# Encoder layer on one core: copies of the turned probabilities spread over two engines, a reordered handover from the output projection to gate/up, and a split low part in down

## The chip, the cores and the metric

The kernel runs on one core of a Trainium2 chip. The metric is the device time of the whole program in microseconds (us); smaller is better. A core has TensorE (PE, matrix products; its weight loads are shown as PEld), VectorE (DVE), ScalarE (ACT), GpSimd (POOL) and SyncE (SP, which issues most DMAs). Each engine works through its own instructions strictly in order; between engines there are semaphores, on which an instruction waits until a count is reached.

## The reference

One layer of a streaming encoder, on 2048 prompt tokens and 8 streams of 16 new tokens (2176 tokens, 1024 wide):

```python
h = rmsnorm(x, norm_mix_pre)
qa, ka, va, logf, qb, kb, vb = project_in(h, w_in, b_forget)
oa = fox_fn(qa, ka, va, logf)          # 8 heads x 64, causal, bias C[t]-C[s]
ob = band_fn(qb, kb, vb)               # 8 heads x 64, own chunk and 8 before it
oa = rmsnorm(oa.reshape(...), gain_out_a)
ob = rmsnorm(ob.reshape(...), gain_out_b)
mix = jnp.concatenate([oa, ob], axis=-1) @ w_out
x = x + rmsnorm(mix, norm_mix_post)
hf = rmsnorm(x, norm_ffn_pre)
ff = (jax.nn.silu(hf @ w_gate) * (hf @ w_up)) @ w_down
x = x + rmsnorm(ff, norm_ffn_post)
```

`attend` inside both heads' functions is softmax(q k / 8 + bias) v.

## The kernel before

Every product with weights is done as three passes: both operands are split into a high part (a rounded copy, type fp32r, made on ACT) and a low part (original minus high, made on DVE or POOL), and PE adds high x high, high x low and low x high. So each operand costs an ACT and a DVE (or POOL) instruction before PE can use it. In names, a final h or l stands for these parts (`ffn_wh`, `ffn_wl`).

The stages follow each other on the one core: the front projections (to about 615 us), attention (615 to 1303), the output projection (1305 to 1535, 17 tiles of 128 tokens, NT = 17), gate and up (1544 to 2492), down (2492 to 3005) and a short tail. The order of each engine's work is written by hand.

**Attention.** PE computes scores (`att_s`, L1077), DVE adds the bias and reduces the row's extreme (L1353), ACT takes the exponential (`exps`, L1219, into `att_sx`), PE turns the probabilities by 64 x 64 transposes (`turn`, L1114 and L1094) into two PSUM banks `pt[0]` and `pt[1]` (both shown as `att_pt`), which are copied to SBUF (`att_pts`), and PE multiplies them with the values (L1152). There are 296 turns. There is one pair of `pt` banks for all of them, so a turn waits until both copies of the turn before are done: `copied(G - 1)` waits on `s_ca` (ACT's copies, L1230) and `s_cd` (DVE's, L1364). The first bank is always copied by ACT. The second is copied by ACT if the next turn comes behind value products (`LONG`, 176 turns: ACT makes both copies, one after the other) and by DVE if it comes right after (120 turns, called split turns here):

```python
def by_dve(G, x):
    return x == 1 and not LONG[G]
```

**The handover to gate/up.** The output projection's last two tiles (x = 15 and 16) pass through group sums (`group_b`, L1792), post-norm (`resid_add`, L1811 and L1817, which ends x1), the norm before gate/up (`second`, `hidden`) and a transpose (L1726) whose result DVE copies out (`mix_hidden`, L1800, `mix_ht`) and SP stores to `mid_hT`. Gate and up are then a Strassen-like product: 3 windows of tokens times 22 weight tiles (`n` from 0 to 65), each with 7 products (`product(n, x)`, x = 0 to 6, PE lines L2179, L2181, L2182) of sums of blocks. The first window's sums and parts are made during the handover: `ffn_sr` (three sums, L2466, L2472, L2486), `high_h(0, x)` on ACT (L2270) and `low_h(0, x)` on DVE (L2412) for x = 0 to 6. For each weight tile POOL makes four sums (`w_sums`, L2093 to L2099, into `ffn_tr`), ACT the high parts (`high_first` L2239, `high_sums` L2245, `high_lower` L2252, `high_up` L2257), DVE the low parts (`low_first` L2389, `low_sums` L2395, `low_lower` L2401, `low_up` L2405). Results meet in DVE's additions u2, u3, c22, c21, c12 (L2505 to L2549). Of what PE waits for: product 3 needs ACT's copy `p1` of product 0's result (`ffn_p`, L2341), product 5 needs u3, product 6 needs c22; product (1, 0) needs the copies of tile 16.

**Down.** 34 tiles; tile n needs `ah[n % 2]` (ACT, L2287) and `al[n % 2]`. Tile 0's low part is made in two halves side by side (POOL L2137, DVE L2511), tile 1's whole by POOL (L2140), the later ones whole by DVE (L2423). There is one landing buffer `ar` for all tiles, loaded by SP's `acts(n)`.

Of the kernel before, what the change touches and what calls it, by code (L numbers as in the profile page):

```python
# [7 lines left out]
ALU = mybir.AluOpType  # L8
# [649 lines left out]
def attend(nc, t, keep, neg_c, recips):  # L658
# [9 lines left out]
    DVES = counted(0 if x else 1 for x in LONG)  # L668
# [25 lines left out]
    with ExitStack() as ctx:  # L694
# [105 lines left out]
        with nc.Block() as block:  # L800
# [236 lines left out]
            def _(pe):  # L1037
# [154 lines left out]
            def _(act):  # L1192
# [29 lines left out]
                def copy(n, g, x):  # L1222
                    G = T0[n] + g
                    if by_dve(G, x):
                        return
# [24 lines left out]
            def _(dve):  # L1250
# [105 lines left out]
                def copy(n, g):  # L1356
                    G = T0[n] + g
                    if not by_dve(G, 1):
                        return
# [514 lines left out]
def output_and_ffn(nc, t, mix_sem, up, down, ahead, recips):  # L1874
# [9 lines left out]
    with ExitStack() as ctx:  # L1884
# [80 lines left out]
        with nc.Block() as block:  # L1965

            @block.sync
            def _(sp):
# [32 lines left out]
                def acts(n):  # L2001
                    if n >= NM:
                        return
                    sp.wait_ge(s_low, min(n, 2))
                    sp.wait_ge(s_al, max(n - 1, 1))
                    act_halves(n)
# [20 lines left out]
                for n in range(NU):  # L2027
# [56 lines left out]
            def _(pool):  # L2084
# [55 lines left out]
                nc.gpsimd.tensor_tensor(al[1][:], ar, f32(ah[1][:]), ALU.subtract).then_inc(s_low, 1)  # L2140
# [6 lines left out]
            def _(pe):  # L2147
# [51 lines left out]
                for n in range(NM):  # L2199
                    c, i = divmod(n, NT)  # L2200
                    u = n % 2
                    out = py[n % NPY][:]
                    if n == 1:
                        pe.wait_ge(s_low, 2)
                    else:
                        pe.wait_ge(s_al, max(n, 1))
# [25 lines left out]
            def _(act):  # L2232
# [95 lines left out]
                act.wait_ge(mix.s_x1, NT)  # L2328
                for n in range(NU):
# [5 lines left out]
                    high_first(n + 1)  # L2335
# [5 lines left out]
                    nc.scalar.activation(p1[:, :w], X[u][:, :w], ACT.Copy).then_inc(s_p1, 1)  # L2341
                    if NU - 6 <= n < NU - 2:
# [8 lines left out]
                    high_sums(n + 1)  # L2351
# [6 lines left out]
                    nc.scalar.activation(sg[:, :w], X[u][:, :w], ACT.Silu).then_inc(s_g1, 1)  # L2358
                    if n == NU - 1:
# [24 lines left out]
            def _(dve):  # L2384
# [74 lines left out]
                group_b(NT - 2, 1)  # L2459
                variance(NT - 1)  # L2460
                resid(NT - 2)
                resid_add(NT - 2)
# [3 lines left out]
                nc.vector.tensor_tensor(sr[:, 0, :, :w], a21, a22, ALU.add).then_inc(s_sd, 1)  # L2466
                group_b(NT - 1, 0)
                low_first(0)
                second(NT - 2)
                mix_hidden(NT - 3)  # L2470
                dve.wait_ge(s_sd, 1)
                nc.vector.tensor_tensor(sr[:, 1, :, :w], sr[:, 0, :, :w], a11, ALU.subtract).then_inc(s_sd, 1)  # L2472
                low_sums(0)
                group_b(NT - 1, 1)
                low_h(0, 0)
                resid(NT - 1)
# [4 lines left out]
                mix_hidden(NT - 2)  # L2481
                dve.wait_ge(mix.sth[1], 16 * len(range(1, NT, 2)))
                low_lower(0)
                low_h(0, 3)
                dve.wait_ge(s_sd, 2)
                nc.vector.tensor_tensor(sr[:, 2, :, :w], a12, sr[:, 1, :, :w], ALU.subtract).then_inc(s_sd, 1)  # L2486
                low_h(0, 4)
                low_h(0, 5)
                mix_hidden(NT - 1)
                low_h(0, 6)  # L2490
                dve.wait_ge(mix.st1[2], 16 * len(range(2, NT, 3)))
                dve.wait_ge(mix.s_h, NT - 2)
                dve.wait_ge(mix.s_th, NT - 1)
# [169 lines left out]
```

## Time and profile before

| | |
|---|---|
| three runs, median | 3031.85 us (3030.17 to 3039.38) |
| the profiled execution | 3030.77 us, of which the span of the trace is 3029.0 us |
| mean granted TensorE clock | 0.981 |
| busy: PE, PEld | 2847.1 us (94%), 2551.3 us (84%) |
| busy: DVE, ACT, POOL | 1632.7 us (54%), 1201.2 us (40%), 752.3 us (25%) |
| shares of the chain that ended last | PE 50%, DVE 3%, issue 1%, DMA 1%, ACT 1% |

PE is busy for 2847.1 of 3029.0 us, so at most some 180 us of idle PE can be won without less PE work; a busy share is a mean over stages with different limits, and what a wait is worth has to be read where it stands. In the rows below, a row of a timeline gives the start, the duration, the engine, the line, and in brackets the idle time ahead of the instruction and what ended it.

### The profile page before, as it was taken

Reading aid. Unit: us, or ns where it says so; the run is one execution under the profiler, and the core shown is the slowest. Engines: PE = TensorE matmul, PEld = TensorE weight load, DVE = VectorE, ACT = ScalarE, POOL = GpSimd, SP = SyncE. Lnnn points to the kernel's source line nnn. Section 1 sums busy time; section 2 is a strip of 40 time slices with the busy share of each in tenths; the row PEclk is TensorE's granted clock in tenths of the full one; section 3 lists DMA queues with packets and bytes.
Section 4 is the critical chain, followed back from the end, with each engine's and each line's share of the span. In section 5 each row is a group of like instructions: output and inputs, shape, how many; then the busy total and the mean of one; then the engine's idle time right before and its main releaser. Section 6 shows DMA issues by size and latency. Waiting matters only on the chain.

```text
span 3029.0 us, 54879 instructions
## 1 busy us (share of the span) xinstructions
PE 2847.1 (94%) x22143; PEld 2551.3 (84%) x22143; DVE 1632.7 (54%) x2945; ACT 1201.2 (40%) x2080; POOL 752.3 (25%) x683
## 2 busy tenths in 40 slices
PE   7999999979999789969979999999999999999998
PEld 7999999957777566758869999999999997887887
DVE  6222121166667456757777667776776662224443
ACT  5330000057777566745543334333433342223221
POOL 0000000055345123023335444543443420000000
PEclk9999999979999999989989999999999999999999
DMA  5322212152112897567723322423223345335553
GB/s 169 96 72 78 76 62 76 48 165 76 63 39 56 256 293 239 152 198 218 242 96 135 112 95 94 152 95 114 89 102 112 128 133 148 96 96 162 165 165 120
DMA packets 285540, 384.75 MB, mean 127 GB/s; under 512 B 24473, under 2 KB 211113, under 8 KB 273513
## 3 DMA queue, kind: packets, MB, share of 16 engines
q1 hardware_dynamic: 284984, 379.68, 39.9%
q8 instruction: 177, 2.90, 0.4%
q10 hardware_dynamic: 304, 1.57, 0.2%
q14 instruction: 75, 0.61, 0.1%
HBM read 291.91 MB, written 89.28 MB: 126 GB/s over the span
## 4 chain that ended last, share of the span: by engine, by line
PE 50%; DVE 3%; issue 1%; DMA 1%; ACT 1%; POOL 0%; SPq 0%; DVEq 0%; POOLq 0%; ACTq 0%
PE ffn_x L2179 3%; PE ffn_w L2179 3%; PE ffn_x L2182 3%; PE ffn_w L2182 3%; PE ffn_x L2181 3%; PE ffn_w L2181 3%; PE ffn_z L2179 3%; PE ffn_z L2182 3%; PE ffn_z L2181 3%; PE ffn_z L2214 1%; PE ffn_z L2216 1%; PE ffn_w L2214 1%; PE ffn_z L2215 1%; PE ffn_w L2216 1%; PE ffn_y L2179 1%
## 5 line engine op out<-in xcount | busy, mean ns | idle before, releaser
L1230 ACT ACTIVATE att_pts<-att_pt 128x384 f32<-128x384 f32 (+3 forms) x472 | 209.7, 483 | 203.9 <-PE att_pt L1114 190.1
L1219 ACT ACTIVATE att_sx<-att_sx,att_nm 128x640 f32<-128x640 f32 (+17 forms) x272 | 264.8, 980 | 6.4 <-DVE att_nm L1353 6.4
L1114 PEld LDWEIGHTS att_pt<-att_eye,att_sx 64*128 64x128 f32 x3296 | 130.7, 140 | 126.5 <-ACT att_pts L1230 66.4
L80 PE MATMUL frt_pz<-frt_xhi,frt_hi 128*128 128x448 f32 (+1 forms) x640 | 230.5, 360 | 0.0
L82 PE MATMUL frt_pz<-frt_xhi,frt_lo 128*128 128x448 f32 (+1 forms) x640 | 230.5, 360 | 0.0
L81 PE MATMUL frt_pz<-frt_xlo,frt_hi 128*128 128x448 f32 (+1 forms) x640 | 230.0, 359 | 0.0
L1114 PE MATMUL att_pt<-att_eye,att_sx 64*128 64x64 f32 x3296 | 168.9, 233 | 63.2 <-ACT att_pts L1230 23.0
L515 DVE TENSOR_TENSOR frt_shared<-frt_pz,frt_rb 128x448 f32<-128x448 f32 (+1 forms) x80 | 48.9, 612 | 313.5 <-PE frt_pz L82 313.5
L1152 PE MATMUL att_po<-att_pts,att_vv 128*64 128x128 f32 x3296 | 217.2, 279 | 0.0
L1152 PEld LDWEIGHTS att_po<-att_pts,att_vv 128*64 128x64 f32 x3296 | 177.9, 137 | 44.7 <-ACT att_pts L1230 25.9
L2179 PE MATMUL ffn_z<-ffn_hh,ffn_wh 128*128 128x362 f32 (+1 forms) x528 | 174.2, 330 | 3.6 <-DVE ffn_u L2515 3.4
L80 PE MATMUL frt_pv<-frt_hi,frt_xhi 128*128 128x256 f32 (+1 forms) x544 | 157.3, 289 | 18.7 <-DVE frt_lo L447 15.8
L2182 PE MATMUL ffn_z<-ffn_hh,ffn_wl 128*128 128x362 f32 (+1 forms) x528 | 173.7, 329 | 0.0
L2181 PE MATMUL ffn_z<-ffn_hl,ffn_wh 128*128 128x362 f32 (+1 forms) x528 | 173.0, 328 | 0.0
L81 PE MATMUL frt_pv<-frt_lo,frt_xhi 128*128 128x256 f32 (+1 forms) x544 | 154.4, 284 | 0.0
L82 PE MATMUL frt_pv<-frt_hi,frt_xlo 128*128 128x256 f32 (+1 forms) x544 | 154.1, 283 | 0.0
L2395 DVE TENSOR_TENSOR ffn_wl<-ffn_tr,ffn_wh 128x2048 fp32r<-128x2048 f32 x66 | 150.8, 2285 | 0.4 <-ACT ffn_wh L2245 0.4
L371 ACT ACTIVATE frt_hi<-frt_raw,frt_gain 128x256 fp32r<-128x256 f32 x96 | 41.4, 497 | 270.8 <-DMA frt_raw<-in_w_slab 270.8
L2423 DVE TENSOR_TENSOR ffn_al<-ahead_first,ffn_ah 128x2816 fp32r<-128x2816 f32 x32 | 99.0, 3093 | 78.9 <-ACT ffn_ah L2287 77.5
L2368 ACT ACTIVATE ffn_c<-ffn_c 128x362 f32<-128x362 f32 (+1 forms) x66 | 33.5, 508 | 252.6 <-DVE ffn_c L2543 252.6
L2144 POOL TENSOR_TENSOR ffn_rr<-ffn_vv,ffn_power 128x1 f32<-128x1 f32 x17 | 9.4, 550 | 499.4 <-DVE ffn_vv L2443 499.4
L2245 ACT ACTIVATE ffn_wh<-ffn_tr 128x2048 fp32r<-128x2048 f32 x66 | 126.1, 1911 | 17.8 <-POOL ffn_tr L2099 17.7
(326 smaller groups left out, 8331.9 us busy)
## 6 DMA issues: line engine op xcount, KB each, us to landing
ahead_first<-mid_act SPq DMA_DIRECT2D x68, 704.0 KB, 6.7
ahead_second<-in_w_gu SPq DMA_DIRECT2D x33, 1024.0 KB, 5.3
ffn_wr<-in_w_gu SPq DMA_DIRECT2D x33, 1024.0 KB, 5.3
att_raw<-out_zT SPq DMA_DIRECT2D x64, 256.0 KB, 4.1
att_bb<-in_cache_ak SPq DMA_DIRECT2D x16, 1024.0 KB, 11.0
att_bb<-in_cache_av SPq DMA_DIRECT2D x16, 1024.0 KB, 9.2
mid_act<-ffn_ao SPq DMA_DIRECT2D x44, 362.0 KB, 2.5
out_zT<-frt_shared SPq DMA_DIRECT2D x64, 224.0 KB, 1.9
```

The lines of the kernel that those rows point to most:

```text
L80: nc.tensor.matmul(out, a_hi(k), b_hi(k), start=(k == 0), stop=False)
L81: nc.tensor.matmul(out, a_hi(k), b_lo(k), start=False, stop=False)
L82: last = nc.tensor.matmul(out, a_lo(k), b_hi(k), start=False, stop=(k == kk - 1))
L1114: last = nc.tensor.transpose(pt[x][:, to:to + 64], sx[n % NSX][r, e, c:c + P], eye[r, r])
L1152: last = nc.tensor.matmul(po[n % 2][r, 0:P], vv[u][:, kt, r], pts[G % NPT][:, e, j, :], start=(g == 0 and j == 0), stop=(g == len(groups) ...
L1219: nc.scalar.activation(sx[n % NSX][:, e, :w], sx[n % NSX][:, e, :w], ACT.Exp, bias=nm[n % NSX][:, e:e + 1], scale=-1.0, accum_out=total).t ...
L1230: nc.scalar.activation(pts[G % NPT][:, :, 0:k, 64 * x:64 * x + 64], pt[x][:].rearrange("p (e j q) -> p e j q", e=2, q=64)[:, :, 0:k, :], A ...
L2179: nc.tensor.matmul(out, high[:, k, :], hh[x][:, k, :w], start=(k == 0 and not more), stop=False, skip_group_check=True)
L2181: nc.tensor.matmul(out, high[:, k, :], hl[x][:, k, :w], start=False, stop=False, skip_group_check=True)
L2182: last = nc.tensor.matmul(out, low[:, k, :], hh[x][:, k, :w], start=False, stop=end, skip_group_check=True)
L2245: nc.scalar.activation(wh[n % 2][:, 1:], tr[:], ACT.Copy).then_inc(ht, 1)
L2395: nc.vector.tensor_tensor(wl[n % 2][:, 1:], tr[:], f32(wh[n % 2][:, 1:]), ALU.subtract).then_inc(lt, 1)
```

## The change

Three edits; nothing of what is computed changes.

A. In attention each turn's second bank is now copied by DVE always, the first by ACT always:

```diff
-    def by_dve(G, x):
-        return x == 1 and not LONG[G]
-
-    def copies(G, dve):
-
-        return DVES[G + 1] if dve else 2 * (G + 1) - DVES[G + 1]
+    def by_dve(x):
+        return x == 1
...
                 def copied(G):
-                    pe.wait_ge(s_ca, copies(G, False))
-                    after(pe, s_cd, copies(G, True))
+                    pe.wait_ge(s_ca, G + 1)
+                    pe.wait_ge(s_cd, G + 1)
```

B. Around the last output tile, POOL makes the first weight tile's sums ahead of tile 16's and tile 15's norm powers, and ACT and DVE are reordered; part of what stood ahead of the loop over weight tiles now stands inside it, at n = 0:

```diff
                 pool.wait_ge(s_pw, 1)
-                rms(NT - 1)
-                post_rms(NT - 2)
                 pool.wait_ge(mix.s_x1, NT - 2)
                 pool.wait_ge(mix.s_ahead, 48)
                 w_sums(0)
+                rms(NT - 1)
+                post_rms(NT - 2)
...
-                first_sum(NT - 2)
                 act.wait_ge(mix.s_ahead, 48)
                 high_first(0)
+                first_sum(NT - 2)
...
-                second_sum(NT - 1)
-                high_lower(0)
-                high_h(0, 3)
-                mix_hidden(NT - 1)
-                for x in range(4, NX):
-                    high_h(0, x)
...
                     nc.scalar.activation(p1[:, :w], X[u][:, :w], ACT.Copy).then_inc(s_p1, 1)
+                    if n == 0:
+                        second_sum(NT - 1)
+                        high_lower(0)
+                        high_h(0, 3)
+                        mix_hidden(NT - 1)
+                        high_h(0, 4)
...
                     nc.scalar.activation(sg[:, :w], X[u][:, :w], ACT.Silu).then_inc(s_g1, 1)
+                    if n == 0:
+                        high_h(0, 5)
+                        high_h(0, 6)
+                        act.wait_ge(mix.s_x1, NT)
+                        high_first(1)
+                        high_sums(1)
...
+                    if n == 0:
+                        dve.wait_ge(s_sd, 2)
+                        nc.vector.tensor_tensor(sr[:, 2, :, :w], a12, sr[:, 1, :, :w], ALU.subtract).then_inc(s_sd, 1)
...
                     if n == 0:
+                        low_h(0, 4)
+                        low_h(0, 5)
+                        mix_hidden(NT - 1)
+                        low_h(0, 6)
                         dve.wait_ge(mix.st1[1], 16 * len(range(1, NT, 3)))
                         dve.wait_ge(mix.s_th, NT)
+                        low_first(1)
                     low_sums(n + 1)
```

C. Down's second low part is made by POOL (upper half) and DVE (lower half), PE and SP wait on both, and SP loads `acts(1)` ahead of weight tiles 18 to 21:

```diff
-                nc.gpsimd.tensor_tensor(al[1][:], ar, f32(ah[1][:]), ALU.subtract).then_inc(s_low, 1)
+                nc.gpsimd.tensor_tensor(al[1][:, js], ar[:, js], f32(ah[1][:, js]), ALU.subtract).then_inc(s_low, 1)
...
+                js = slice(0, NJ // 2)
+                dve.wait_ge(s_ah, 1)
+                nc.vector.tensor_tensor(al[1][:, js], ar[:, js], f32(ah[1][:, js]), ALU.subtract).then_inc(s_al, 1)
...
+                acts(1)
                 for q in range(18, NJ):
                     down_weights(q)
-                acts(1)
```

What this moves is seen in the order of the instructions. ACT in the middle of attention: `att_pts` rows are the copies, `att_sx` rows the exponentials, xN is a run of N alike. Before:

```order
L1230 ACTIVATE att_pts<-att_pt 128x8x64
L1230 ACTIVATE att_pts<-att_pt 128x2x3x64 x2
L1219 ACTIVATE att_sx,att_sums<-att_sx,att_nm 128x1280
L1230 ACTIVATE att_pts<-att_pt 128x2x3x64 x3
L1219 ACTIVATE att_sx,att_sums<-att_sx,att_nm 128x1280
L1230 ACTIVATE att_pts<-att_pt 128x2x3x64 x2
L1219 ACTIVATE att_sx,att_sums<-att_sx,att_nm 128x1408
```

The same place after (its L1225 is the L1230 of before, its L1214 the L1219):

```order
L1225 ACTIVATE att_pts<-att_pt 128x8x64
L1225 ACTIVATE att_pts<-att_pt 128x2x3x64
L1214 ACTIVATE att_sx,att_sums<-att_sx,att_nm 128x1280
L1225 ACTIVATE att_pts<-att_pt 128x2x3x64 x2
L1214 ACTIVATE att_sx,att_sums<-att_sx,att_nm 128x1280
L1225 ACTIVATE att_pts<-att_pt 128x2x3x64
L1214 ACTIVATE att_sx,att_sums<-att_sx,att_nm 128x1408
```

Where ACT made two copies between exponentials it now makes one; DVE has one copy row more for each of these turns. DVE around the end of tile 15, before (`mix_x` is x1 of tile 15, `ffn_sr` the sums, the last row the low part of the first product's operand):

```order
L1792 SCALAR_TENSOR_TENSOR mix_y_20915<-ffn_w,mix_r_20932,mix_ta_20910 128x512
L1784 TENSOR_SCALAR mix_ss_20929<-ffn_z 128x2
L1807 TENSOR_SCALAR mix_s_20934<-mix_s_20934 128x1
L1811 SCALAR_TENSOR_TENSOR mix_y_20915<-mix_y_20915,mix_r_20936,mix_g_post 128x1024
L1817 TENSOR_TENSOR mix_x_20911<-mix_y_20915,mix_xr_20916 128x1024
L2466 TENSOR_TENSOR ffn_sr<-ahead_first 128x4x362
L1792 SCALAR_TENSOR_TENSOR mix_y_20914<-ffn_y,mix_r_20931,mix_ta_20909 128x512
L2389 TENSOR_TENSOR ffn_wl_20866<-ahead_second,ffn_wh_20864 128x512
...
L2412 TENSOR_TENSOR ffn_hl_20878<-ahead_first,ffn_hh_20871 128x4x362
```

And after:

```order
L2463 TENSOR_TENSOR ffn_sr<-ahead_first 128x4x362
L1787 SCALAR_TENSOR_TENSOR mix_y_20915<-ffn_w,mix_r_20932,mix_ta_20910 128x512
L1779 TENSOR_SCALAR mix_ss_20929<-ffn_z 128x2
L2390 TENSOR_TENSOR ffn_wl_20866<-ahead_second,ffn_wh_20864 128x512
L1802 TENSOR_SCALAR mix_s_20934<-mix_s_20934 128x1
L1806 SCALAR_TENSOR_TENSOR mix_y_20915<-mix_y_20915,mix_r_20936,mix_g_post 128x1024
L1812 TENSOR_TENSOR mix_x_20911<-mix_y_20915,mix_xr_20916 128x1024
L1787 SCALAR_TENSOR_TENSOR mix_y_20914<-ffn_y,mix_r_20931,mix_ta_20909 128x512
...
L2413 TENSOR_TENSOR ffn_hl_20878<-ahead_first,ffn_hh_20871 128x4x362
```

The first `ffn_sr` sum and the low part `ffn_wl` have moved ahead of the end of x1. ACT around the first weight tile, before (`ffn_hh` are the high parts for products 3 to 6, `ffn_p` is p1, `ffn_sg` the gate):

```order
L2252 ACTIVATE ffn_vh<-ahead_second 128x512
L2270 ACTIVATE ffn_hh_20874<-ahead_first 128x4x362
L1643 ACTIVATE mix_h_20919<-mix_x_20912,mix_r_20939 128x1024
L2270 ACTIVATE ffn_hh_20875<-ffn_sr 128x4x362
L2270 ACTIVATE ffn_hh_20876<-ahead_first 128x4x362
L2270 ACTIVATE ffn_hh_20877<-ffn_sr 128x4x362
L2257 ACTIVATE ffn_vh<-ahead_second 128x512
L2239 ACTIVATE ffn_wh_20865<-ffn_wr_20862 128x512
L2341 ACTIVATE ffn_p_20885<-ffn_x 128x362
```

And after:

```order
L2251 ACTIVATE ffn_vh<-ahead_second 128x512
L2329 ACTIVATE ffn_p_20885<-ffn_x 128x362
L1632 ACTIVATE mix_h_20919,mix_s_20937<-mix_x_20912 128x1024
L2246 ACTIVATE ffn_vh<-ahead_second 128x512
L2264 ACTIVATE ffn_hh_20874<-ahead_first 128x4x362
L1638 ACTIVATE mix_h_20919<-mix_x_20912,mix_r_20939 128x1024
L2264 ACTIVATE ffn_hh_20875<-ffn_sr 128x4x362
L2353 ACT_TABLE_LOAD
L2353 ACTIVATE ffn_sg<-ffn_x 128x362
```

`ffn_p` has moved from behind all the `ffn_hh` and the next weight tile's `ffn_wh` to ahead of them.

## Rows read from the trace of the kernel before

**Rows 1.** Waits of PE, whole run: us in total, times, longest.

```profile
PE att_pt L1114 <- ACT att_pts L1230: 23.0, 36, 1.3
...
PE att_pt L1114 <- ACT att_sx L1219: 14.3, 19, 4.7
PE att_pt L1114 <- DVE att_pts L1364: 12.3, 17, 2.0
...
PE att_pt L1094 <- ACT att_sx L1219: 1.7, 3, 0.9
```

**Rows 2.** Groups by line from 600 to 1640 us: xcount, busy, mean ns.

```profile
L1230 ACT ACTIVATE att_pts<-att_pt 128x384 f32<-128x384 f32 (+3 forms) x472 | 209.7, 483 | 203.9 <-PE att_pt L1114 190.1 <-PE att_pt L1094 13.6
...
L1364 DVE COPY att_pts<-att_pt 128x384 f32<-128x384 f32 (+2 forms) x120 | 70.2, 585 | 47.0 <-PE att_pt L1114 45.0
```

**Rows 3.** Timeline of ACT and PE around one split turn.

```profile
895.86 1.09 ACT L1230 ACTIVATE att_pts<-att_pt 128x512 f32<-128x512 f32 x2 [0.91 <-PE att_pt L1114]
896.83 2.00 ACT L1219 ACTIVATE att_sx<-att_sx,att_nm 128x2048 f32<-128x2048 f32 x1
...
898.82 0.60 ACT L1230 ACTIVATE att_pts<-att_pt 128x512 f32<-128x512 f32 x1
...
899.47 0.34 PE L1114 MATMUL att_pt<-att_eye,att_sx 64*128 64x64 f32 x4 [1.32 <-ACT att_pts L1230]
```

**Rows 4.** Timeline of PE, the start of attention.

```profile
621.09 0.75 PE L1114 MATMUL att_pt<-att_eye,att_sx 64*128 64x64 f32 x4 [4.17 <-ACT att_sx L1219]
```

**Rows 5.** Timeline of DVE, ACT and PE around one LONG turn in the band heads.

```profile
1162.73 0.61 DVE L1353 CUSTOM_DVE_ANT_0 att_sx<-att_s,att_brel,att_nm 128x384 f32<-128x384 f32 x1
...
1163.02 1.08 ACT L1230 ACTIVATE att_pts<-att_pt 128x512 f32<-128x512 f32 x2 [0.91 <-PE att_pt L1094]
...
1164.49 0.22 PE L1094 MATMUL att_pt<-att_eye,att_sx 64*16 64x64 f32 x2
```

**Rows 6.** Timeline of PE in the handover to gate/up.

```profile
1543.85 0.64 PE L2179 MATMUL ffn_x<-ffn_hh,ffn_wh 128*128 128x362 f32 x1 [5.89 <-issue]
...
1563.06 0.64 PE L2179 MATMUL ffn_x<-ffn_hh,ffn_vh 128*128 128x362 f32 x1 [10.30 <-ACT ffn_p L2341]
...
1572.78 0.64 PE L2179 MATMUL ffn_z<-ffn_hh,ffn_wh 128*128 128x362 f32 x1 [3.36 <-DVE ffn_u L2515]
...
1578.35 0.33 PE L2179 MATMUL ffn_x<-ffn_hh,ffn_wh 128*128 128x362 f32 x1
```

**Rows 7.** Timeline of DVE in the handover.

```profile
1522.62 0.75 DVE L1792 SCALAR_TENSOR_TENSOR mix_y<-ffn_w,mix_r,mix_ta 128x512 f32<-128x512 f32 x1 [3.26 <-issue]
...
1529.86 2.75 DVE L2466 TENSOR_TENSOR ffn_sr<-ahead_first 128x1448 f32<-128x1448 f32 x1
...
1555.20 1.72 DVE L2401 TENSOR_TENSOR ffn_vl<-ahead_second,ffn_vh 128x512 fp32r<-128x512 f32 x1 [3.56 <-DMA mid_hT<-mix_ht]
...
1558.42 1.65 DVE L2486 TENSOR_TENSOR ffn_sr<-ahead_first,ffn_sr 128x1448 f32<-128x1448 f32 x1
...
1567.49 0.69 DVE L1800 TENSOR_TENSOR mix_ht<-ffn_x,mix_g_ffn 128x512 f32<-128x512 f32 x1 [4.26 <-PE ffn_y L1726]
```

**Rows 8.** Timeline of POOL in the handover, the first sum of weight tile 1.

```profile
1551.04 1.30 POOL L2093 TENSOR_TENSOR ffn_tr<-ffn_wr 128x512 f32<-128x512 f32 x1
```

**Rows 9.** Two stretches: length, then busy us (xcount) of PE, PEld, DVE, ACT, POOL; granted clock, DMA share, GB/s.

```profile
1543.74:1574.76 31.02, 17.04 (x75) 16.25 (x76) 22.18 (x23) 15.71 (x17) 6.15 (x6) 0.72 0.32 110
2514.40:2518.60 4.20, 4.12 (x10) 3.27 (x11) 0.00 (x0) 0.00 (x0) 0.03 (x1) 0.55 0.64 178
```

**Rows 10.** Timelines of POOL, DVE and PE at down's tiles 0 and 1.

```profile
2481.35 3.25 POOL L2137 TENSOR_TENSOR ffn_al<-ahead_first,ffn_ah 128x1408 fp32r<-128x1408 f32 x1 [15.97 <-ACT ffn_ah L2303]
...
2482.53 3.55 DVE L2511 TENSOR_TENSOR ffn_al<-ahead_first,ffn_ah 128x1408 fp32r<-128x1408 f32 x1
...
2508.32 6.11 POOL L2140 TENSOR_TENSOR ffn_al<-ahead_first,ffn_ah 128x2816 fp32r<-128x2816 f32 x1 [23.72 <-ACT ffn_ah L2287]
...
2514.48 0.80 PE L2214 MATMUL ffn_y<-ffn_dh,ffn_ah 128*128 128x512 f32 x1 [7.44 <-POOL ffn_al L2140]
```

More of the change, by code:

```diff
@@ L667, in attend @@
     LONG = [bool(VALUES[x]) for x in TURNS[1:]] + [True]
-    DVES = counted(0 if x else 1 for x in LONG)
     LONGS = [[g for g in range(len(job_groups(n))) if LONG[T0[n] + g]] for n in range(NJOB)]
@@ L1223, in copy @@
                     G = T0[n] + g
-                    if by_dve(G, x):
+                    if by_dve(x):
                         return
@@ L1357, in copy @@
                     G = T0[n] + g
-                    if not by_dve(G, 1):
+                    if not by_dve(1):
                         return
@@ L2004, in acts @@
                     sp.wait_ge(s_low, min(n, 2))
-                    sp.wait_ge(s_al, max(n - 1, 1))
+                    sp.wait_ge(s_al, n)
                     act_halves(n)
@@ L2202, in _ @@
                     out = py[n % NPY][:]
+                    pe.wait_ge(s_al, n + 1)
                     if n == 1:
                         pe.wait_ge(s_low, 2)
-                    else:
-                        pe.wait_ge(s_al, max(n, 1))
                     if n >= NPY:
@@ L2319, in _ @@
                 high_h(0, 2)
-                second_sum(NT - 1)
-                high_lower(0)
-                high_h(0, 3)
-                mix_hidden(NT - 1)
-                for x in range(4, NX):
-                    high_h(0, x)
                 act.wait_ge(mix.st1[2], 16 * len(range(2, NT, 3)))
                 act.wait_ge(mix.s_th, NT - 1)
-                act.wait_ge(mix.s_x1, NT)
                 for n in range(NU):
@@ L2334, in _ @@
                     high_up(n)
-                    high_first(n + 1)
+                    if n >= 1:
+                        high_first(n + 1)
                     if n == NU - 1:
@@ L2350, in _ @@
                         high_h(p + 1, 0)
-                    high_sums(n + 1)
+                    if n >= 1:
+                        high_sums(n + 1)
                     if end:
@@ L2458, in _ @@
                 group_b, variance, resid, resid_add, second, mix_hidden = mix.vector(dve)
[L2459 to L2462, printed above, removed]
                 dve.wait_ge(mix.s_sq, NT)
@@ L2466, in _ @@
                 nc.vector.tensor_tensor(sr[:, 0, :, :w], a21, a22, ALU.add).then_inc(s_sd, 1)
+                group_b(NT - 2, 1)
+                variance(NT - 1)
+                low_first(0)
+                resid(NT - 2)
+                resid_add(NT - 2)
                 group_b(NT - 1, 0)
-                low_first(0)
                 second(NT - 2)
                 mix_hidden(NT - 3)
+                low_sums(0)
                 dve.wait_ge(s_sd, 1)
                 nc.vector.tensor_tensor(sr[:, 1, :, :w], sr[:, 0, :, :w], a11, ALU.subtract).then_inc(s_sd, 1)
-                low_sums(0)
                 group_b(NT - 1, 1)
                 low_h(0, 0)
+                mix_hidden(NT - 2)
                 resid(NT - 1)
@@ L2480, in _ @@
                 second(NT - 1)
[L2481 to L2490, printed above, removed]
                 dve.wait_ge(mix.st1[2], 16 * len(range(2, NT, 3)))
@@ L2493, in _ @@
                 dve.wait_ge(mix.s_th, NT - 1)
+                dve.wait_ge(mix.sth[1], 16 * len(range(1, NT, 2)))
                 for n in range(NU):
@@ L2499, in _ @@
                     low_up(n)
-                    low_first(n + 1)
+                    if n == 0:
+                        low_lower(0)
+                        low_h(0, 3)
+                    else:
+                        low_first(n + 1)
                     dve.wait_ge(s_p1, n + 1)
@@ L2505, in _ @@
                     nc.vector.tensor_tensor(u2[:, :w], p1[:, :w], Y[u][:, :w], ALU.add).then_inc(s_add, 1)
+                    if n == 0:
+                        dve.wait_ge(s_sd, 2)
+                        nc.vector.tensor_tensor(sr[:, 2, :, :w], a12, sr[:, 1, :, :w], ALU.subtract).then_inc(s_sd, 1)
                     if end:
```

## The prediction

> **What bounds the kernel now.** I read the page first: PE is busy for 94% of the span, so a change that takes no work from PE can only win PE's idle time, and only where PE waits for what the change moves. So I went next to PE's waits over the whole run and then, for the three places the change touches, to the timelines of all engines there.
>
> In attention the reader is to see in [rows 1] that PE waits 23.0 us for ACT's copies of turned P (36 times), 12.3 us for DVE's copies (17 times) and 14.3 + 1.7 us for exponentials; in [rows 2] that ACT makes 472 copies of 0.48 us, DVE 120 of 0.59. In the handover to gate/up there are four gaps of PE, of which [rows 6] shows the three that matter after the first product may start: 5.89 us ahead of it, 10.30 for p1, 3.36 for u3. In down one gap of 7.44 us for tile 1's low part [rows 10]. After such gaps PE runs slow for a while: behind the 7.44 us the granted clock of the next 4.20 us is 0.55 [rows 9], the lower of its two levels, so a removed gap gives back some of that too.
>
> **Part A, the copies.** 176 copies move from ACT to DVE. What would be the direct gain is that a LONG turn's pair, one behind the other on ACT for 1.08 or 1.09 us [rows 3, 5], becomes two copies side by side of about 0.6. I went through every stall of PE on a copy in order of time: all of them stand behind split turns, which already have one copy on each engine; none stands behind a LONG turn, since there PE has value products to do meanwhile (in [rows 5] the pair ends at 1164.10 and the next turn starts at 1164.49). So the direct gain is zero, hidden by the value products. An indirect gain is left: ACT comes to its next work 0.49 us earlier (1.09 less the single copy's 0.60). [Rows 3] shows how that reaches PE: the pair ends at 896.92, the exponential of 2.00 runs until 898.82, and only then comes the split turn's copy, for whose end PE waits 1.32. This figure comes four times, 92 us apart, from 715.62 to 991.42. Four times 0.49 is 2.0. I estimate the shorter stalls of the same kind, nine of them, at 2.4. Then the waits for exponentials: 14.3 + 1.7 less the two at the start of attention (4.17 in [rows 4] and the longest one, 4.7), where no turn stands ahead, leaves 7.1 which an ACT with 176 x 0.48 = 85 us less to do could take away. The upper bound is so 2.0 + 2.4 + 7.1 = 11.5. The lower is zero: where ACT is earlier the turn may then wait for scores or DVE instead. The stalls on exponentials lie mostly in the band heads, where DVE's bias work comes ahead of the exponential and is itself late, so that I take 60%: **-7 us**.
>
> What A costs: DVE gets 176 x 0.6 = 106 us more, in 690 us of attention. A copy queued on DVE stands behind bias work and ahead of it. At the tightest LONG turn [rows 5] DVE is free at 1163.34 (and then has short bias work), the turned P is there at 1163.02, and a copy of 0.61 would end at 1163.95 or a little later, 0.5 before the next turn. The bias work behind it comes 0.6 later, and after that the scores that wait for its banks. If that cover goes, each such turn costs up to what a present wait for DVE costs, 12.3/17 = 0.72 us. I take no cost into the sum, and up to 3 us into the range.
>
> **Part B, the handover.** PE's order is unchanged; the chain runs through DVE. (1) Ahead of the first product DVE is idle for 3.26 us [rows 7], which sr's first sum now fills; it leaves the stretch behind x1 of tile 15, where it took 2.75. The low part of the first weight block also moves ahead, about 1 us; x1 ends perhaps 0.3 later, since ACT's and POOL's steps for it stand behind the weight tile's, and the rest may collide with POOL. I take -2.5 for the start of the first product: 1543.85 becomes 1541.35.
>
> (2) From there to c22, which releases product 6, DVE's list of work is the same before and after, only in another order. Before, this stretch ran from 1543.74 to 1574.76: 31.02 us, DVE busy for 22.18 [rows 9]. Of its idle 8.84, 3.56 us are the wait for tile 15's store to land and 4.26 the wait for PE's transpose of tile 16, which itself stood behind PE's wait of 10.30 for p1 [rows 6, 7]. The first goes, since the copy of tile 15's transposed hidden now stands ahead of the first x1 step of tile 16 and its store has more than 5 us to land; the second goes, since p1 no longer stands behind all of ACT's high parts and the copy of tile 16 has moved behind u3. That is -7.8.
>
> (3) What is added: POOL's four sums for weight tile 1, 4 x 1.30 = 5.2 us from 1551.04 on [rows 8], ran mostly beside the idle 3.56. Now DVE has work all along. That the two disturb each other shows in [rows 7]: the same shape of 1448 elements took 2.75 beside POOL's sums and 1.65 without. The trace bounds the cost between nothing and 5.2; since part of DVE's work there reads PSUM and some of POOL's time falls on waits, I take about half, +2.5.
>
> The sum: c22 starts at 1574.76 - 2.5 - 7.8 + 2.5 = 1567.0 and ends at 1567.4. Product 6 then takes 3.3 after a wait (products 5 and 6 of before took 5.57 together, 1572.78 to 1578.35, the first of them at the low clock; at the high one a product takes 2.0). Product (1, 0) so starts at 1570.7 instead of 1578.35: **-7.6 us**. Without any collision and at the high clock it would be -11.4, with the whole 5.2 and half of the 4.26 kept, about -3: those are the bounds.
>
> The Trainium skill, "SBUF — State Buffer", sections "SBUF: two separate sides" and "Who interferes with whom", says that a DVE instruction with two SBUF inputs and a GpSimd instruction that reads SBUF exclude one another for the whole of an instruction. By that B's collision would be the whole 5.2 and B -4.9; the 2.75 against 1.65 agrees that they disturb each other, but shows 1.1 lost beside sums that ran for all of it.
>
> **Part C, down's second low part.** Now 2816 elements take POOL 6.11 [rows 10]. How long the two halves take side by side is shown at tile 0: POOL 3.25 from 2481.35, DVE 3.55 from 2482.53, both done at 2486.08. DVE ended 1.48 after POOL, so they took turns rather than running together, 4.73 from the start. So -1.4, and the load moved ahead of four weight tiles gives a little where it was late, but the high part of tile 1 still stands behind the last weights' high parts on ACT: I take **-1.5**, between 0 (the DVE half queued late) and -3 (side by side, 3.1 instead of 6.11). The slow clock behind the gap stays.
>
> **Sum.** -7 - 7.6 - 1.5 = -16.1 against the profiled execution of 3030.77: 3014.7. The median of the three runs is 1.1 above that execution, so I forecast 3015.8.
>
> **Rivals.** 0.3%, about what a measurement of this kernel tells from no change, is 9.1 us here.
>
> 1. Forecast: all three pay roughly as worked out, 3010 to 3021. Chance 0.50.
> 2. The gain is eaten by POOL and DVE taking turns. POOL's sums for weight tiles 0 and 1 and its subtraction now fall on dense DVE work; with the whole 5.2 lost, B gives -4.9; and if A's earlier ACT only brings the four stalls like [rows 3] (2.0) and C 1.4, the sum is -8.3, so about 3023.5; 3021 to 3027 in all. For it: the 2.75 in [rows 7]. Against: of the 8.84 us idle most is a wait for events that are plainly moved. Chance 0.24. The skill's rule on the shared port pair, cited above, is this case.
> 3. More: A's waits for exponentials go entirely (-11.5) and B runs free of collisions (-11.4), with C -3, 3005 to 3010. Chance 0.16.
> 4. The change does not do what it says in attention: the waits in [rows 1] stay, since they stand behind turns that are split already, and the handover wins only the start, 2.5; 3027 to 3030. Chance 0.05.
> 5. Slower: DVE works in order, so the 176 new copies delay the bias work of the job behind them, hence its exponentials, hence PE. At the present price of a wait for DVE, 0.72, B and C (9.1) are used up after 13 of the 176 turns, and with no gain from A the run is slower by 0.3% after 25. For it: in [rows 5] the slack is half a microsecond. Against: this is the tightest one that I found, and DVE has no more than a pair of bias steps ahead of a copy. Chance 0.05.
>
> The range 3004 to 3027 reaches from the third case's lower part to the second's upper end and leaves out the fourth and fifth and the extremes of the third. Faster by over 0.3% (under 3022.7): 0.50 + 0.16 + 0.10 of the second = 0.76; the same: 0.14 + 0.05 = 0.19; slower 0.05.
>
> **What would show each step.** A: the wait of PE for ACT's copies falls from 23.0 to about 18, the wait for exponentials from 16.0 towards 11 to 12, and the wait for DVE's copies stays near 12; if DVE's bias row or its copies show up as a new wait of PE with dozens of occurrences, the step is wrong. B: the first product at 1541 to 1542 (on the old time scale, attention's gain taken off), no 10.30 ahead of product 3, no idle DVE of 3.56 and 4.26, and product (1, 0) about 29 us behind the first product's start, against 34.5 before; DVE's durations longer than 1.65 for 1448 elements show the collision. C: the gap at tile 1 is 5 to 6 us instead of 7.44. The prediction is wrong if the gap at p1 turns up again elsewhere on PE, at u3 or c22 say, at its full length.

## The result, and the profile after

The changed kernel took 3012.01 us (median of 4 runs, 3007.07 to 3012.93) beside 3031.01 for the kernel before: ratio 0.993, 95% interval 0.9907 to 0.9952, so 15 to 28 us faster. The forecast was 3015.8, and the result lies in the forecast's own case (3010 to 3021), near its lower end. Run again beside later experiments it took 3011.85, ratio 0.9923 (0.991 to 0.9937). The profiled execution took 3007.07 us, span 3005.3, which is 23.7 under the span of before; it was the fastest of its four, so that 23.7 is more than the 19.0 between the medians.

Waits of PE over the whole run, after (us in total, times, longest), which answer to [rows 1]; lines have moved by 5 or more, so L1109 is the L1114 of before, L1225 the L1230, L1359 the L1364, L1214 the L1219:

```profile
PE att_pt L1109 <- ACT att_pts L1225: 18.3, 31, 0.8
...
PE att_pt L1109 <- DVE att_pts L1359: 15.6, 18, 4.7
...
PE att_pt L1109 <- ACT att_sx L1214: 5.6, 4, 4.6
PE ffn_y L2208 <- POOL ffn_al L2135: 5.5, 1, 5.5
...
PE att_pt L1089 <- ACT att_sx L1214: 0.5, 1, 0.5
```

The wait for ACT's copies fell from 23.0 to 18.3 and its longest from 1.3 to 0.8; the waits for exponentials from 16.0 to 6.1. The wait for DVE's copies rose from 12.3 to 15.6, but its longest, 4.7, is the wait at 630 us at the start of attention, which before was put down to an exponential (the 4.7 in [rows 1]); without it 10.9 are left, and with it the waits for exponentials are 10.8 instead of 16.0.

To see where the 23.7 us went, I cut the run at instructions of PE that both kernels have. Timeline of PE, after: the first score, the first product of the output projection, product (0, 0), product (1, 0), down's tile 2.

```profile
614.78 0.47 PE L1072 MATMUL att_s<-att_kh,att_qh 64*128 64x128 f32 x2 [7.83 <-DVE att_ql L1254]
...
1307.33 0.77 PE L1741 MATMUL ffn_x<-mix_wh,mix_oh 128*128 128x512 f32 x1 [20.35 <-DVE mix_ol L1764]
...
1528.21 0.64 PE L2174 MATMUL ffn_x<-ffn_hh,ffn_wh 128*128 128x362 f32 x1 [4.96 <-issue]
...
1556.29 0.50 PE L2174 MATMUL ffn_x<-ffn_hh,ffn_wh 128*128 128x362 f32 x1
...
2509.22 0.40 PE L2208 MATMUL ffn_z<-ffn_dh,ffn_ah 128*128 128x512 f32 x1
```

Differences of such starts in us, for the two kernels and for the parts run alone (the experiments below); "attention" ends with the first product of the output projection and so holds the wait of some 20 us ahead of that, and "down" is from the start of tile 0 to that of tile 2:

| run | attention | output projection | product (0, 0) to (1, 0) | down |
|---|---|---|---|---|
| before | 705.84 | 222.74 | 34.50 | 39.65 |
| after | 692.55 | 220.88 | 28.08 | 38.83 |
| after, again | 696.73 | 221.28 | 28.20 | 39.04 |
| A alone | 695.55 | 223.72 | 34.91 | 39.42 |
| B alone | 706.14 | 219.43 | 29.00 | 39.83 |
| C alone | 710.69 | 226.59 | 34.91 | 38.32 |

Attention and the output projection, where nothing differs, vary by 4 to 5 us from run to run (705.84 to 710.69 with unchanged copies; C alone was profiled in the slowest of its eleven executions), the last two columns by up to 1.6. So small parts are read from the stages, not from the time. All fourteen traces of this document, cut in the same way, tell more than the six: attention takes 705.8 to 710.7 in the three with the copies of before and 692.5 to 699.1 in the nine with A's, and down 39.4 to 40.8 in the five without C and 38.3 to 39.0 in the five that have C as in the change.

The handover after, on PE, DVE and POOL (timelines), for [rows 6 to 8]:

```profile
1539.49 0.44 PE L2174 MATMUL ffn_x<-ffn_hh,ffn_vh 128*128 128x362 f32 x1 [1.64 <-DVE ffn_hl L2413]
...
1544.82 0.67 PE L2174 MATMUL ffn_w<-ffn_hh,ffn_wh 128*128 128x362 f32 x1 [2.16 <-DVE ffn_hl L2413]
...
1553.59 0.40 PE L2174 MATMUL ffn_w<-ffn_hh,ffn_vh 128*128 128x362 f32 x1 [3.08 <-DVE ffn_c L2537]
```

```profile
1536.97 2.47 DVE L2413 TENSOR_TENSOR ffn_hl<-ahead_first,ffn_hh 128x1448 fp32r<-128x1448 f32 x1 [0.20 <-ACT ffn_hh L2264]
...
1539.80 2.30 DVE L2505 TENSOR_TENSOR ffn_sr<-ahead_first,ffn_sr 128x1448 f32<-128x1448 f32 x1
...
1544.69 2.74 DVE L2413 TENSOR_TENSOR ffn_hl<-ahead_first,ffn_hh 128x1448 fp32r<-128x1448 f32 x1
...
1548.55 1.65 DVE L2413 TENSOR_TENSOR ffn_hl<-ffn_sr,ffn_hh 128x1448 fp32r<-128x1448 f32 x1
...
1552.93 0.52 DVE L2537 TENSOR_TENSOR ffn_c<-ffn_u,ffn_w 128x362 f32<-128x362 f32 x1
```

```profile
1537.99 2.59 POOL L2090 TENSOR_TENSOR ffn_tr<-ffn_tr,ffn_wr 128x512 f32<-128x512 f32 x1
```

The wait of 10.30 for p1 and DVE's idle 3.56 and 4.26 are gone. Product 3 waits 1.64 for an operand, product 4 2.16, product 6 3.08 for c22: DVE's list of work is now what PE follows. And the collision is plain: while POOL makes its sums (2.59 where [rows 8] has 1.30), DVE's 1448 elements take 2.3 to 2.7, and 1.65 once POOL is done.

Down's tile 1 after, DVE, POOL and PE (timelines), for [rows 10]:

```profile
2486.71 1.63 DVE L2570 TENSOR_TENSOR ffn_al<-ahead_first,ffn_ah 128x1408 fp32r<-128x1408 f32 x1 [1.75 <-ACT ffn_ah L2281]
```

```profile
2486.82 4.52 POOL L2135 TENSOR_TENSOR ffn_al<-ahead_first,ffn_ah 128x1408 fp32r<-128x1408 f32 x1 [23.61 <-ACT ffn_ah L2281]
...
2491.49 0.76 PE L2208 MATMUL ffn_y<-ffn_dh,ffn_ah 128*128 128x512 f32 x1 [5.47 <-POOL ffn_al L2135]
```

Both halves start together. DVE takes 1.63, POOL 4.52, which is 1.5 more than half of the 6.11 of a whole one [rows 10] and so about the time that DVE works: 4.6 in all, as forecast. The gap is 5.47 instead of 7.44.

### The profile page after: what moved, and what is told of

Read it like the earlier page. It is cut to its first block, busy times and chain, and to the rows that moved or that the text cites. A ratio compares the mean times of both kernels' runs of the same rounds, so it can differ in the third digit from the quotient of the medians.

```text
span 3005.3 us, 54881 instructions
## 1 busy us (share of the span) xinstructions
PE 2845.9 (95%) x22143; PEld 2552.1 (85%) x22143; DVE 1709.5 (57%) x3122; ACT 1139.9 (38%) x1904; POOL 754.4 (25%) x683
## 4 chain that ended last, share of the span: by engine, by line
PE 44%; issue 6%; DVE 3%; POOL 2%; DMA 1%; ACT 1%; SPq 0%; POOLq 0%; DVEq 0%; ACTq 0%
PE ffn_w L2174 3%; PE ffn_x L2174 3%; PE ffn_w L2177 3%; PE ffn_x L2177 3%; PE ffn_w L2176 3%; PE ffn_x L2176 3%; PE ffn_z L2177 3%; PE ffn_z L2174 3%; PE ffn_z L2176 3%; PE ffn_z L2208 1%; PE ffn_w L2208 1%; PE ffn_y L2174 1%; PE ffn_w L2210 1%; PE ffn_z L2210 1%; PE ffn_y L2177 1%
## 5 line engine op out<-in xcount | busy, mean ns | idle before, releaser
L1214 ACT ACTIVATE att_sx<-att_sx,att_nm 128x640 f32<-128x640 f32 (+17 forms) x272 | 263.4, 971 | 7.4 <-DVE att_nm L1348 7.4
L1225 ACT ACTIVATE att_pts<-att_pt 128x384 f32<-128x384 f32 (+3 forms) x296 | 145.3, 491 | 251.3 <-PE att_pt L1109 236.6
L1109 PEld LDWEIGHTS att_pt<-att_eye,att_sx 64*128 64x128 f32 x3296 | 129.9, 140 | 115.7 <-ACT att_pts L1225 60.1
L1109 PE MATMUL att_pt<-att_eye,att_sx 64*128 64x64 f32 x3296 | 166.5, 232 | 55.2 <-ACT att_pts L1225 18.3
L1359 DVE COPY att_pts<-att_pt 128x384 f32<-128x384 f32 (+3 forms) x296 | 164.3, 555 | 64.6 <-PE att_pt L1109 58.4
```

The costliest lines, as they stand in the source:

```text
L1109: last = nc.tensor.transpose(pt[x][:, to:to + 64], sx[n % NSX][r, e, c:c + P], eye[r, r])
L1214: nc.scalar.activation(sx[n % NSX][:, e, :w], sx[n % NSX][:, e, :w], ACT.Exp, bias=nm[n % NSX][:, e:e + 1], scale=-1.0, accum_out=total).t ...
L1225: nc.scalar.activation(pts[G % NPT][:, :, 0:k, 64 * x:64 * x + 64], pt[x][:].rearrange("p (e j q) -> p e j q", e=2, q=64)[:, :, 0:k, :], A ...
L1359: nc.vector.tensor_copy(pts[G % NPT][:, :, 0:k, 64:128], pt[1][:].rearrange("p (e j q) -> p e j q", e=2, q=64)[:, :, 0:k, :]).then_inc(s_c ...
```

## The experiments

The theory from the prediction: A wins because ACT reaches its queued work earlier; B because DVE's idle time goes, less a collision with POOL; C little, since the two engines take turns. The main rival for A: a turn's pair of copies simply ends sooner on two engines.

**The three parts alone.** Each kernel is the one before with one of the three edits of the diff above.

> The kernel before with the copies of turned P alone changed (first bank ACT, second DVE, at every turn). If the parts add up and the forecast's size is right: 7 us faster, attention from the first score to the first product of the output projection 706 us before, 699 here. If the 13 us that this stretch lost in the profile of the changed kernel are the part's own: 692 to 694. If most of those 13 us are one run's luck: 698 or more. A cost on DVE would show as more wait of PE for DVE's bias work (4.5 us before).

> The kernel before with the handover to gate/up alone reordered. Forecast: 7.6 us faster, product (1, 0) 29 us behind the first product instead of 34.5, and the first product 2.5 us earlier behind the output projection's start. In the profile of the changed kernel the two were 6.4 and 1.9. If the gain needs the changed attention (it should not), less than 4.

> The kernel before with down's second low part alone split and its load moved ahead. Forecast: 1.5 us faster, gap of PE at tile 1 about 6 us instead of 7.44; the two engines taking turns would give 4.5 to 4.7 for both halves together, side by side 3.2. By the time alone this can't be told from no change.

A alone: 3024.44 us beside 3031.65, ratio 0.9976 (0.9967 to 0.9985), 4.5 to 10 us faster; its attention took 695.55, between the two first cases that were expected. B alone: 3024.61, ratio 0.997 (0.9958 to 0.9982), 5.5 to 12.7 faster, and it needs nothing from A. C alone: 3031.93, ratio 1.0005 (0.9996 to 1.0014), no change that the time can tell; by the stage 38.32 instead of 39.65, 1.3 us. The medians of the parts add up to 14, which is less than the 19.0 and 21.3 of the whole. In the table the parts alone are worth 10.3 (attention), 8.8 (output projection and handover) and 1.3 (down), together 20.4, where the same columns give 22.4 and 17.5 for the whole; so no part is seen to help another, and why the medians of A alone and B alone give less than their stages stays open.

Within attention the 272 exponentials of ACT are finer marks. From the 31st to the 136th, all in the FoX heads, it took 311.41 us before and 310.31 in the run of B alone, against 301.84 after and 302.03 with A alone: 9.4 us with a scatter of 1. From the 196th to the 272nd, in the band heads: 140.47 and 140.52 against 138.72 and 138.45, 2 us.

**The pair on one engine.** At LONG turns DVE makes both copies:

```diff
-    DVES = counted(0 if x else 1 for x in LONG)
+    DVES = counted(2 if x else 1 for x in LONG)
...
-        return x == 1 and not LONG[G]
+        return x == 1 or LONG[G]
```

> The kernel before, but at the 176 turns where ACT made both copies DVE makes both, one after the other; the split turns stay as they are. The pair so ends no sooner than before (two of 0.6 us in a row), but ACT has 352 copies fewer. If the gain of the copies comes from ACT reaching its exponentials and its split-turn copies earlier (forecast): as fast as the split alone or faster, 7 to 14 us under before. If it comes from the pair ending sooner because it runs on two engines: no gain, 0 to 3 us slower than before. If DVE's load is what counts: slower than before by over 5, with waits of PE for DVE's bias work.

Measured: 3037.08, ratio 1.0027 (1.0017 to 1.0038), slower by 5 to 12 us. That is the third case. The time alone would not tell what became of ACT's side. Waits of PE, whole run (L1114 turn, L1364 DVE's copies, L1353 its bias work):

```profile
PE att_pt L1114 <- DVE att_pts L1364: 24.9, 29, 5.6
...
PE att_pt L1114 <- ACT att_pts L1230: 19.2, 35, 0.8
...
PE att_s L1077 <- DVE att_nm L1353: 9.3, 18, 3.4
...
PE att_pt L1114 <- ACT att_sx L1219: 3.7, 1, 3.7
```

ACT's side has the whole gain of A without the pair ending sooner (19.2 and 0.8 longest; exponentials only the one wait at the start), but the waits for DVE's copies and bias work are 14 us more than with A alone (24.9 and 9.3 beside 15.1 and 5.1). One copy more per turn DVE has room for, two it has not.

**ACT kept as late as before.** A alone, but ACT does small copies of a constant in place of the one it gave away, so that only the two-engine pair is left of A:

```diff
                     if by_dve(x):
+                        if LONG[G]:
+                            act.wait_ge(s_tr, G + 1)
+                            for c in range(2):
+                                after(act, s_dm, len(extra))
+                                extra.append(c)
+                                nc.scalar.activation(scr[:], eye[:, 0:64], ACT.Copy).then_inc(s_dm, 1)
                         return
```

> The copies alone changed, as in e1_copies, but at the 176 turns ACT does two small copies of a constant (64 elements each) in place of the copy it gave away, so that it reaches its next work about as late as before, while the pair of copies still runs on two engines at once. If e1's gain comes from ACT reaching its exponentials and split-turn copies earlier: most of it is gone, 0 to 3 us faster than before, with waits of PE for exponentials back (3.1 us in the FoX heads before, none in e1). If it comes from the pair ending sooner: 6 to 8 us faster, as e1.

Measured: 3036.2, ratio 1.0012 (1.0003 to 1.0021): all of the gain is gone, and a little more. Group of these copies by line, and waits of PE (L1111 the turn, L1233 ACT's copies, L1216 the exponential):

```profile
L1228 ACT ACTIVATE att_scr<-att_eye 128x64 bf16<-128x64 f32 x352 | 89.1, 253 | 5.6
```

```profile
PE att_pt L1111 <- ACT att_pts L1233: 28.1, 51, 1.3
...
PE att_pt L1111 <- ACT att_sx L1216: 12.0, 23, 5.0
```

Two of them cost 0.51 us per turn, about the 0.49 that A takes from ACT. The longest wait for a copy is back at 1.3 and the waits for exponentials at 12.0 in 23 places; attention takes 710.75, and from the 31st exponential to the 136th it is 310.63 again. The waits for ACT's copies, 28.1, are above the 23.0 of before, so the dummies hold ACT up a little longer than the copies did, and by the time alone a small gain of the pair could hide behind that. The trace of before leaves no room for one: each of its 53 waits for a copy (36 for ACT's, 17 for DVE's) stands at a turn without value products ahead of it, so behind a turn that was split already. So it is ACT's time that A wins by; the pair side by side wins nothing.

**The collision, taken away.** After, but POOL's sums for weight tile 1 run over one column only:

```diff
+                    if n == 1:
+                        b11, b21, b12, b22 = (b[:, :, 0:1] for b in (b11, b21, b12, b22))
+                        tr = tr_all[:, :, :, 0:1]
```

> The changed kernel, but POOL's four sums for weight tile 1 are made for one column in 128 only (these sums are left out, so tile 1 of gate/up is computed from other numbers); all else is as in the changed kernel. It measures what POOL beside dense DVE work costs in the handover. Product (1, 0) stood 28.08 us behind the first product. My half of POOL's 5.2 us: 25.5. The whole lock by the rule on the shared port: 23. If the collision costs nothing there: 28. DVE's 1448-element instructions should all take 1.65 instead of 2.3 to 2.7.

Measured: product (1, 0) 26.18 behind the first product, 1.9 less; DVE as expected (timeline):

```profile
1545.07 1.65 DVE L2511 TENSOR_TENSOR ffn_sr<-ahead_first,ffn_sr 128x1448 f32<-128x1448 f32 x1
...
1548.88 1.67 DVE L2419 TENSOR_TENSOR ffn_hl<-ahead_first,ffn_hh 128x1448 fp32r<-128x1448 f32 x1
...
1556.04 0.53 DVE L2543 TENSOR_TENSOR ffn_c<-ffn_u,ffn_w 128x362 f32<-128x362 f32 x1
```

c22 starts 21.75 us behind the first product (1556.04 less 1534.29) instead of 24.72 (1552.93 less 1528.21): the collision costs DVE's chain 3.0 us. This is sharp: in the five traces with the handover as in the change (the two of the whole, B alone, and, further below, the half wait and the low part on DVE) c22 starts 24.71 to 24.73 behind the first product. That product (1, 0) comes only 1.9 earlier can't be put down to the edit: product 6 took 3.8 us instead of 2.7, but in those five traces it took anything from 2.05 to 3.61, as more or fewer of its matmuls ran at the lower level of the clock (0.50 instead of 0.33 us each).

**c22 first, and PE's half wait.** Both are edits of the changed kernel. In the first DVE makes c22 of weight tile 0 ahead of the low parts of tile 1; in the second PE starts down's tile 1 on DVE's half:

```diff
-                        low_first(1)
-                    low_sums(n + 1)
+                    else:
+                        low_sums(n + 1)
...
                     nc.vector.tensor_tensor(c22[:, :w], u3[:, :w], W[u][:, :w], ALU.add).then_inc(s_add, 1)
+                    if n == 0:
+                        low_first(1)
+                        low_sums(1)
```

```diff
-                    if n == 1:
-                        pe.wait_ge(s_low, 2)
...
-                        if n == 0 and j == NJ // 2:
-                            pe.wait_ge(s_low, 1)
+                        if n <= 1 and j == NJ // 2:
+                            pe.wait_ge(s_low, n + 1)
```

> The changed kernel, but DVE makes c22 of weight tile 0 ahead of the low parts of weight tile 1 (0.68 and 2.28 us). If product 6's new wait of 3.08 us for c22 is DVE's order, as read from the trace: the wait falls to about 0.2 and product (1, 0) comes 25 us behind the first product instead of 28.08. If DVE's low parts are the bound of what follows, the wait moves to product (1, 0) or (1, 1) and the stage is as long.

> The changed kernel, but PE starts down's tile 1 when DVE's half of the low part is there and waits for POOL's half only at the middle of the tile (as it does at tile 0). DVE's half ended 3.15 us before PE started. Expected: PE's gap at tile 1 falls from 5.47 to about 2.3, and from tile 0's start to tile 2's start 35.5 instead of 38.8; if POOL's half then stalls the middle, 37.

c22 first: product (1, 0) 24.65 behind the first, better than expected, with 1.04 left of the wait. But one weight tile later PE waits again for c22 (timeline):

```profile
1555.46 0.40 PE L2174 MATMUL ffn_w<-ffn_hh,ffn_vh 128*128 128x362 f32 x1 [1.04 <-DVE ffn_c L2537]
...
1571.46 0.50 PE L2174 MATMUL ffn_w<-ffn_hh,ffn_vh 128*128 128x362 f32 x1 [1.86 <-DVE ffn_c L2537]
```

There c22 again stands behind the next tile's low parts, and these behind a weight load that has only just landed; so of the 3.4 us at least this wait was given back. How much in all isn't shown: from the first product to down it was 940.93 us instead of 942.18, but the four traces with the changed kernel's own gate/up (its two, the half wait and the low part on DVE) have 940.3 to 943.3. The half wait did what was expected: tile 0 to tile 2 34.42 instead of 38.83 (one run, 3006.98), and the gap (timeline) is 2.31:

```profile
2492.58 0.50 PE L2206 MATMUL ffn_y<-ffn_dh,ffn_ah 128*128 128x512 f32 x1 [2.31 <-DVE ffn_al L2568]
```

**All of the second low part on DVE.** After, with POOL's half given to DVE:

```diff
-                nc.gpsimd.tensor_tensor(al[1][:, js], ar[:, js], f32(ah[1][:, js]), ALU.subtract).then_inc(s_low, 1)
...
-                nc.vector.tensor_tensor(al[1][:, js], ar[:, js], f32(ah[1][:, js]), ALU.subtract).then_inc(s_al, 1)
+                nc.vector.tensor_tensor(al[1][:], ar, f32(ah[1][:]), ALU.subtract).then_inc(s_al, 1)
```

> The changed kernel, but DVE makes all of down's second low part and POOL none. In the changed kernel the halves ended 4.6 us after their start (DVE 1.63, then POOL until 4.52), though a whole one takes DVE 3.09 by itself later on. If the two engines take turns: done after 3.1, PE's gap at tile 1 falls from 5.47 to about 4.0. If they work side by side and POOL is simply slow: POOL's half should have taken 3.2, and this would win 0.1 only.

Measured (timelines of DVE and PE): one engine is quicker than the two, 3.09 against 4.6, and the gap 3.81.

```profile
2492.16 3.09 DVE L2565 TENSOR_TENSOR ffn_al<-ahead_first,ffn_ah 128x2816 fp32r<-128x2816 f32 x1 [1.75 <-ACT ffn_ah L2276]
...
2495.31 0.50 PE L2203 MATMUL ffn_y<-ffn_dh,ffn_ah 128*128 128x512 f32 x1 [3.81 <-DVE ffn_al L2565]
```

**A better version, and one step too far.** The first of three kernels on one chip is the changed kernel itself. The second has c22 ahead of the low parts for weight tiles 0 to 2, and the half wait. The third also moves, on ACT and DVE, the high part of down's tile 1 and its half low part ahead of those of weights 18 to 21 (`high_a(1)` between `high_w(17)` and `high_w(18)`).

> The changed kernel itself once more, beside the next two on one chip. The parts alone gave 7.2, 7.0 and about 0 us by their medians, 1.2 for the third by its stage: if they add up, 14 to 16 us faster than before; if together they are worth more, 19 or more.

> The changed kernel with c22 ahead of the next weight tile's low parts for weight tiles 0 to 2 (not for tile 0 alone, after which the wait came back one tile later, 1.86 us and a low clock) and with the half wait at down's tile 1. If both waits are DVE's and PE's order and nothing else is late: from the first product to down's first matmul 938.5 instead of 942.2, from tile 0 to tile 2 of down 34.4 instead of 38.8, together about 8 us faster than the changed kernel. If c22's place only moves the wait on to weight tile 3 or to product (n, 1): 4 to 5.

> As e10, and ACT makes the high part of down's tile 1 (and DVE its half of the low part) ahead of those of weights 18 to 21, since its load is now issued ahead of theirs. If the load has landed by then: PE's gap at tile 1 falls from 2.3 to under 0.5, 1.5 to 2 us faster than e10. If it lands later than the weights, PE waits for weights 18 to 21 inside tile 0 instead: as long as e10 or longer.

Measured: 3011.85, ratio to before 0.9923 (0.991 to 0.9937); 3003.04, ratio 0.9898 (0.9885 to 0.9912); 3012.7, ratio 0.9929 (0.9917 to 0.9942). The first, 21.3 us under before, lies in the second case of its expectation, though the stages of the parts show no such help (above). The second is 8.8 us faster than the first by the medians (2999.33 to 3004.46 beside 3007.03 to 3014.84), as expected: from the first product to down 937.43, without the wait of 1.86 one weight tile later, and tile 0 to tile 2 34.37. The third is no faster than the changed kernel (timelines of ACT and PE):

```profile
2485.97 2.56 ACT L2279 ACTIVATE ffn_ah<-ahead_first 128x2816 fp32r<-128x2816 f32 x1 [6.32 <-DMA ahead_first<-mid_act]
...
2493.80 0.79 PE L2206 MATMUL ffn_x<-ffn_dh,ffn_ah 128*128 128x512 f32 x1 [5.76 <-DVE ffn_dl L2418]
```

The load lands 10.45 us after tile 0 starts (2475.52), so ACT waits 6.32 for it, the weights' parts behind it are late, and PE stands 5.76 inside tile 0. That is the second case expected, and it costs 4.2 us (38.61 from tile 0 to tile 2). The rest of the 9.7 between the medians isn't explained by it: in this trace the stretch from the first product to down, where nothing but the last steps ahead of down differs from the second kernel, took 941.29.

## Why the prediction was right, step by step

**A, -7.** The mechanism was right: no gain from the pair, the whole gain from ACT's 0.49 per turn. The four stalls like [rows 3] show it to the digit, 1.32 before and 0.83 or 0.84 after; one of them:

```profile
892.46 0.71 PE L1109 MATMUL att_pt<-att_eye,att_sx 64*128 64x64 f32 x16 [0.83 <-ACT att_pts L1225]
```

The wait for ACT's copies was forecast at 18 and is 18.3. The term that was mis-sized is the share of 60%. The prediction's signs take it of the 7.1 of exponentials alone (16.0 to 11 or 12), which with 2.0 and 2.4 for the copies would have given -8.7; its -7 is 60% of the whole 11.5. Of the 7.1, 5.6 went (1.5 left beside the 4.6 at the start), and with the 4.7 of the copies that is 10.3 of 11.5. 3.1 of the 5.6 stood in the FoX heads, where I had seen little. The stretches between exponentials give 11 for A, and the means of attention in the nine traces with A's copies and the three without lie 11.8 apart, a little over the upper bound; by A's own time the part is 7.2 (4.5 to 10). So the close match of that time with the -7 is in part luck. PE's matmuls in attention also became shorter by 3.4 in sum (604.76 to 601.39 us busy), which was no term of mine; B alone, with the copies of before, has 602.52, so that at least part of it is scatter. That DVE's copy costs nothing held; the pair on DVE shows that the room is for one copy, not two.

**B, -7.6.** By its time 7.0, or 5.5 to 12.7 by the interval. The first product came 1.9 (after) and 3.3 (alone) earlier, forecast 2.5; the stretch to product (1, 0) shrank by 6.4 and 5.5, forecast 5.1; product 6 alone, by its clock, moves that by 1 or more. The collision was put at 2.5 and is 3.0. The Trainium skill ("SBUF — State Buffer", "Who interferes with whom") calls the port pair that DVE and GpSimd share an exclusive lock; the prediction's estimate from that rule was the whole 5.2 that POOL's sums take by themselves. Tile 1 of down agrees with the rule for a pair of instructions (POOL 4.52 beside DVE's 1.63). In the row of the handover both get longer, POOL's four sums to 9.1 in all and DVE's four instructions of 1448 elements by 3.2, which looks like taking turns. The 5.2 was too much at least because not all of POOL's work meets a DVE instruction with both inputs in SBUF: while the sums run, DVE also stands idle for 0.20 us and makes two additions of 0.52 that read a product's result from PSUM. Whether this is the whole difference between 5.2 and 3.0 isn't shown.

**C, -1.5.** 1.3 by the stage alone, 0.8 and 0.6 in the two runs of the whole, and 1.3 between the means of the five traces with it and the five without; the halves take turns as read from tile 0. The load moved ahead won nothing, though a little was expected of it: tile 1's high part ended 16.3 us after tile 0 began after (2486.67 less 2470.39) as before (2508.18 less 2491.77: 16.4). ACT no longer waits for it (4.14 before), but for the weights issued behind it, 5.93 instead of at most 2.37, and in the second run of the whole PE stood 1.55 inside tile 0 for the weights behind it.

**The sum** of -16.1 was too small by 3 to 5 beside the two measurements of the whole (-19.0 and -21.3). By the stages A was worth 3 to 5 more than I gave it, which is as much as is missing; by its own time it was worth nothing more, and that difference stays open.

## What to carry to other kernels

Before moving work off an engine that is not the bound, look for what stands queued behind it: the gain is the time by which that work comes earlier, and only where the bound engine waits for it (some 85 us taken off ACT were worth 7 to 12 here); a dummy of the same length in the old place shows whether it is that. On an in-order engine, put the instruction that another engine waits for ahead of the preparation for the next round, in each of the first rounds and not only where the wait is seen. Splitting an elementwise step over DVE and POOL when both read SBUF can be slower than DVE alone; a consumer that can start on the first half wins more.

## What had not been expected of the hardware

The DVE and POOL instructions that meet each other both become longer: 1448 elements on DVE 2.3 to 2.7 us instead of 1.65, 512 on POOL 2.59 instead of 1.30. Down's tile 1, loaded in two transfers of 704 KB and issued ahead of four weight tiles of 256 KB, landed only 10.45 us after tile 0 began in the one run that shows it. With this load ahead of them, ACT's longest wait for those weights was 5.8 to 8.0 us in the eight traces with the changed order of loads and ACT's order as in the change, against 1.6 to 2.4 in the five with the old order of loads.
